# Experts' weights in transfers of 2 MB into pairs of raw slots, in place of 1 MB into one

## The chip, the core and the metric

The kernel runs on one core of a Trainium2 chip. Its engines have instruction queues of their own: TensorE (PE; its weight loads are PEld), VectorE (DVE), ScalarE (ACT), GpSimd (POOL) and SyncE (SP, which here only issues DMAs); sixteen DMA engines move data between the chip's memory (HBM) and the core's on-chip memory (SBUF, 128 partitions). Engines wait for one another by semaphores. The time is the device time of one execution in microseconds, as the median of several runs.

## The reference

The input x has 256 rows of 1024 values, all float32. Two blocks of two layers each follow one another. The part that the change touches is the mixture of experts in the second layer of the first block:

```python
def swiglu(x, w_gate, w_up, w_down):
    return (jax.nn.silu(x @ w_gate) * (x @ w_up)) @ w_down

def moe_swiglu(x, w_router, w_gate, w_up, w_down):
    logits = (x @ w_router).astype(jnp.float32)
    top_v, top_i = lax.top_k(logits, TOP_K)          # 2 of 8 experts per row
    top_w = jax.nn.softmax(top_v, axis=-1)
    gates = jnp.sum(jax.nn.one_hot(top_i, N_EXPERTS, dtype=jnp.float32) * top_w[..., None], axis=-2)
    out = jnp.zeros_like(x)
    for e in range(N_EXPERTS):
        out = out + gates[..., e:e + 1] * swiglu(x, w_gate[e], w_up[e], w_down[e])
    return out
```

Each expert has w_gate and w_up of 1024 x 3584 and w_down of 3584 x 1024. The other three layers have attention or a gated delta rule, and dense gated feed-forward parts.

## The kernel before

All weights come as a stream of units. A unit is 128 partitions x 2048 float32, 1 MB, 8 KB in each partition, and lies in HBM as one contiguous block. The stages of a unit are:

1. SyncE issues its DMA into one of six slots of `raw` (`RAW = 6`, line 41), slot `i % RAW` for unit number i. Before the issue it waits until VectorE has done with the unit that was in the slot, number i - 6.
2. ScalarE rounds it into `w_hi` (float32r, `split_hi`, line 521). It waits for the landing of the unit (`wait_loaded`) and for TensorE to be done with the unit three before, since `w_hi` and `w_lo` have three slots (`SPLIT = 3`).
3. VectorE takes the difference `raw - w_hi` into `w_lo` (`split_lo`, line 526) and so frees the raw slot.
4. TensorE multiplies with three products per block, w_hi x_hi, w_lo x_hi and w_hi x_lo (line 771).

A unit's slot is thus requested anew as soon as VectorE's subtraction is over. Each raw slot has a semaphore `loaded`, which a transfer raises by 16.

The expert stage is a hardware loop of eight turns, one per expert, on every engine; the units of a turn are always the same 42 (`EXPERT`, `TURN`). In a step, one for each 512 of the 3584 hidden units, there are two units of w_gate (`wu_eg`), two of w_up (`wu_eu`) and, for the hidden units of an earlier step, two of w_down (`wu_ed`); seven such steps make 42 units, with the down units shifted by two steps, so that the last six units of a turn are all of w_down. The units of one kind come in twos, numbers (f, 0) and (f, 1), and lie next to each other in HBM. The number of units of a turn is a multiple of `RAW`, so the slots are the same in each turn.

TensorE computes gate and up for 128 gathered rows, ScalarE the SiLU (line 1551), VectorE the product (line 2161), TensorE turns it (line 1055), ScalarE and VectorE make its two parts (lines 1561 and 2168), and TensorE multiplies by w_down.

On SyncE's queue stand two more transfers of 512 KB in each turn: before unit 12 (`PUT_AT`) the store of the previous expert's result `ye` to `y_by_expert` (line 588), and before unit 20 (`GET_AT`) the load of the next expert's rows `xt` (line 592). Towards the end of the stage GpSimd gathers rows of `y_by_expert` (line 676).

There is a second path (`overflow_loads`, and the tag `V`) for experts with more than 128 rows. It does not run with these inputs.

The first expert unit has number `expert_base` = 67, the first unit behind the experts has number `after` = 403, so slots are counted from an odd number. The weights for the next stage (`wu_pg`) go on in the same ring of slots.

Of the kernel before, what the change touches and what calls it, by code (L numbers as in the profile page):

```python
# [22 lines left out]
F32 = mybir.dt.float32  # L23
I32 = mybir.dt.int32
ALU = mybir.AluOpType
# [12 lines left out]
NE = 8  # L38
UNIT = 2048
WARM_START, WARM_LN, WARM_RMS = 6, 5, 4  # L40
RAW = 6
# [181 lines left out]
def build_program(nc, A, plan, debug=None):  # L223
    cst_np, cst_at = constants()
    NC = cst_np.shape[1]
    with ExitStack() as ctx:
# [230 lines left out]
            return out + down(EXP_STEPS - 1)  # L457
        EXPERT = expert_order()
        TURN = len(EXPERT)
        assert TURN % RAW == 0 and TURN % SPLIT == 0  # L460
        unit_at, n = {}, 0
        for key, arr, idx in stream_order():
            if key == ("experts",):
# [13 lines left out]
        def place(i):  # L477
            return split_no(i) % SPLIT

        def key_of(i):  # L480
# [2 lines left out]
                return expert_base + TURN + i - after  # L483
            return i

        def wait_loaded(E, eng, i):
            slot, n = i % RAW, 16 * (i // RAW + 1)
            if E.ev.turn is not None:
                n = n + E.ev.turn * (16 * TURN // RAW)
            eng.wait_ge(E.loaded[slot].sem, n)  # L490
            return raw[:, slot, :]
# [31 lines left out]
        def split_lo(E, ve, i):  # L523

            ve.wait_ge(*E.hi.at("unit", i))
            nc.vector.tensor_tensor(w_lo[:, place(i), :], raw[:, i % RAW, :], w_hi[:, place(i), :].bitcast(F32), ALU.subtract) \  # L526
                .then_inc(*E.lo.mark("unit", i))

        def ahead(E, split, eng, key, base=None):
# [21 lines left out]
        @block.sync  # L551
        def _(sp):

            def overflow_loads():
                sp.wait_ge(*flag_done.at())
                r = sp.value_load(flag_i[0:1, 0:1], min_val=0, max_val=1)
                with sp.If(r > 0):
                    sp.wait_ge(*M.put.at("last"))
                    sp.dma_start(yg_own[0, P:S, :], moe["ye"]).then_inc(*V.put.mark("first"))
                    for i in range(after, after + RAW):  # L560
                        wait_loaded(M, sp, i)
                    with sp.Fori(0, NE) as e:
                        with V.ev.loop(e):
                            sp.wait_ge(V.groups.sem, e * plan.per.get("ovf_groups", 0) + 1)
                            for j, (ekey, earr, eidx) in enumerate(EXPERT):
                                if j >= RAW:
                                    sp.wait_ge(*V.lo.at("unit", j - RAW))
                                sp.dma_start(raw[:, j % RAW, :], A[earr][e, eidx[0], eidx[1]]) \
                                    .then_inc(*V.loaded[j % RAW].mark())
                            sp.wait_ge(*V.free[1].at("ovf", "ye", 1))  # L570
                            sp.dma_start(yg_own[e, P:S, :], moe["ye"]).then_inc(*V.put.mark("own"))
                    for i, (arr, idx) in zip(range(after, after + RAW), again):
                        sp.dma_start(raw[:, i % RAW, :], A[arr][idx] if len(idx) > 1 else A[arr][idx[0]]) \
                            .then_inc(*V.loaded[i % RAW].mark("again"))
                    sp.wait_ge(*V.lo.at("again", SPLIT - 1))

            again = [(arr, idx) for key, arr, idx in stream_order() if arr and after <= unit_at[key] < after + RAW]
            sp.dma_start(Rf, A["xT"].rearrange("p c n -> p (c n)")).then_inc(*first_x.mark())
            for key, arr, idx in stream_order():
                if key == ("experts",):  # L580
                    with sp.Fori(0, NE) as e:
                        with ev.loop(e):
                            for j, (ekey, earr, eidx) in enumerate(EXPERT):
                                i = expert_base + j
                                if j == PUT_AT:
                                    sp.wait_ge(*M.dve.at("moe", "zeroed"))
                                    sp.wait_ge(*turn_before(M.free[1], "moe", "ye", 1))
                                    sp.dma_start(yg_before[e, 0:P, :], moe["ye"]).then_inc(*M.put.mark("before"))
                                if j == GET_AT:
                                    sp.wait_ge(*xg_put.at("all"))  # L590
                                    sp.wait_ge(*turn_before(M.groups, "moe", "next", "ga", 1))
                                    sp.dma_start(moe["xt"], xg_next[e, 0:P, :]).then_inc(*xt_in.mark("next"))

                                sem, v = M.lo.at("unit", expert_base + (j - RAW) % TURN)
                                sp.wait_ge(sem, v - plan.per.get("lo_ready", 0) if j < RAW else v)
                                sp.dma_start(raw[:, i % RAW, :], A[earr][e, eidx[0], eidx[1]]) \
                                    .then_inc(*M.loaded[i % RAW].mark())
                    continue
                if unit_at[key] == after + RAW:
                    sp.wait_ge(*M.free[1].at("moe", "ye", 1))  # L600
                    sp.dma_start(yg[NE * S:NE * S + P, :], moe["ye"]).then_inc(*M.put.mark("last"))
                    overflow_loads()
                    for t in range(NT):
                        sp.wait_ge(*high_in[t].at(t))
                i = unit_at[key]
                if i >= RAW:
                    old = i - RAW
                    if expert_base <= old < after:
                        old = expert_base + (old - expert_base) % TURN
                    sp.wait_ge(*(reader(M, old) if old in whole else M.lo.at("unit", key_of(old))))  # L610
                src = A[arr][idx] if len(idx) > 1 else A[arr][idx[0]]
                sp.dma_start(raw[:, i % RAW, :], src).then_inc(*M.loaded[i % RAW].mark())
            for t in range(NT):
                sp.wait_ge(*x_ready.at(3, "ffn", t))
                sp.dma_start(A["out"][t * P:(t + 1) * P, :], X[:, t, :]).then_inc(*stored.mark(t))
            sp.wait_ge(*stored.last())
# [116 lines left out]
        def _(pe):  # L733
# [560 lines left out]
            for L in range(2):  # L1294
                if L == 0:
                    pe.wait_ge(*consts.at())
                    keep_warm(WARM_START, 6)
                    pe.wait_ge(*xs_ready.at("first"))
                mixer(L)
                turn_tile((L, "mix"), 0, lambda t: x_ready.at(L, "mix", t))  # L1300
                keep_warm(WARM_LN, 6)
                turn_tile((L, "mix"), 1, lambda t: x_ready.at(L, "mix", t))
                if L == 0:
                    dense_ffn(0)
                else:
                    router()
                    gather(M, "moe", "first")
                    pe.wait_ge(*flag_done.at())
                    r = pe.value_load(flag_i[0:1, 0:1], min_val=0, max_val=1)
                    gathered(M, "moe", "first")  # L1310
                    with pe.Fori(0, NE) as e:
                        with ev.loop(e):
                            experts(M, "moe", expert_base)
                    with pe.If(r > 0):
                        with pe.Fori(0, NE) as e:
                            with V.ev.loop(e):
                                experts(V, "ovf", 0)
                        for h in range(2):
                            pe.wait_ge(*V.free[h].at("ovf", "ye", h))
                        pe.wait_ge(*V.lo.at("again", SPLIT - 1))  # L1320
                        for i in range(after, after + RAW):
                            pe.wait_ge(*V.loaded[i % RAW].at("again"))

                embedding_gate(L)
            for L in range(2, 4):
# [21 lines left out]
        def _(ac):  # L1347
# [351 lines left out]
            for L in range(2):  # L1699
# [22 lines left out]
                else:  # L1722
# [20 lines left out]
                    with ac.If(r > 0):  # L1743
# [2 lines left out]
                                experts(V, "ovf", 0)  # L1746
                        ac.wait_ge(*V.groups.at("ovf", "dn", EXP_STEPS - 1))
                        for i in range(after, after + RAW):
                            ac.wait_ge(*V.loaded[i % RAW].at("again"))
                        for i in range(SPLIT):  # L1750
                            nc.scalar.copy(w_hi[:, place(after + i), :], raw[:, (after + i) % RAW, :]) \
                                .then_inc(*V.hi.mark("again", i))
                    want_root()
                    norm_root(L, "ffn", 0)
# [58 lines left out]
        def _(ve):  # L1813
# [602 lines left out]
            for L in range(2):  # L2416
# [38 lines left out]
                else:  # L2455
# [15 lines left out]
                    with ve.If(r > 0):  # L2471
# [6 lines left out]
                        for i in range(SPLIT):  # L2478
                            u = after + i
                            ve.wait_ge(*V.hi.at("again", i))  # L2480
                            V_.tensor_tensor(w_lo[:, place(u), :], raw[:, u % RAW, :], w_hi[:, place(u), :].bitcast(F32), ALU.subtract) \
                                .then_inc(*V.lo.mark("again", i))

                    def take_rows(t, nb):
# [177 lines left out]
```

## Time and profile before

| | |
|---|---|
| median of 3 runs | 2253.78 us (2248.89 to 2256.55) |
| the profiled execution | 2255.73 us, span of its instructions 2253.9 us |
| TensorE busy in the span | 2183.6 us (97%) |
| VectorE, ScalarE busy | 1699.0 us (75%), 1385.0 us (61%) |
| moved by the weight queue of SyncE | 545.82 MB in the whole program |
| expert loop | about 500 to 1440 us of the span |

The numbers of the profile come from one execution. "Busy" counts the time in which an engine executes; TensorE's matmuls overlap and their ends are modelled. "Waited for" names what ended an engine's idle time. The rows below are given as the profile has them, grouped by view.

### The profile page before, as it was taken

The numbers are of one execution on the slowest core, as the hardware profiler recorded it, in microseconds if no ns is written. First come the engines' busy times: TensorE is split into PE (matmuls) and PEld (weight loads), VectorE is DVE, ScalarE is ACT, GpSimd is POOL, SyncE is SP. The second block draws the span as 40 slices with busy tenths as digits, with TensorE's granted clock in tenths as the row PEclk, the third lists the DMA queues.
The fourth block names the chain that finished last, engine by engine and source line by source line (L and its number), as shares of the span: only waits on it lengthen the run. The fifth ranks groups of instructions, "written<-read, shape, count | busy, mean of one in ns | idle before, by whom it ended". The sixth has DMA issues, their size and how long they took to land.

```text
span 2253.9 us, 32351 instructions
## 1 busy us (share of the span) xinstructions
PE 2183.6 (97%) x12324; PEld 1870.6 (83%) x12324; DVE 1699.0 (75%) x1888; ACT 1385.0 (61%) x1455; POOL 56.6 (3%) x72
## 2 busy tenths in 40 slices
PE   8899999889999999999999999989999999999998
PEld 6699997668888888888888887769979998988998
DVE  5745457768888888888888889857677777776766
ACT  5543334647777777787777777646465446555444
POOL 2000000020000000000000003000000000000000
PEclk9999999989999999999999999989999999999999
DMA  9555555349999999999999999834135554233551
GB/s 388 217 198 185 187 182 181 119 160 386 373 384 374 385 370 386 374 372 383 366 391 360 395 358 395 327 142 155 68 122 199 178 190 147 93 122 135 184 189 55
DMA packets 81800, 573.35 MB, mean 254 GB/s; under 512 B 9553, under 2 KB 9665, under 8 KB 15985
## 3 DMA queue, kind: packets, MB, share of 16 engines
q1 hardware_dynamic: 76320, 545.82, 64.3%
q0 software_dynamic: 5376, 26.12, 3.1%
q8 instruction: 70, 1.15, 0.2%
q14 instruction: 34, 0.27, 0.0%
HBM read 564.03 MB, written 17.83 MB: 258 GB/s over the span
## 4 chain that ended last, share of the span: by engine, by line
PE 87%; DVE 5%; ACT 5%; issue 2%; DMA 1%; ACTq 0%; DVEq 0%; POOLq 0%
PE bank L771 78%; ACT w_hi L521 2%; DVE w_lo L526 2%; PE bank L1055 1%; PE bank L1180 1%; PE bank L1190 1%; ACT arena L1390 1%; PE bank L1095 1%; DVE R L1885 1%; PE bank L749 1%; PE bank L766 1%; PE bank L835 0%; PE bank L827 0%; DVE arena L1905 0%; DMA cst<-in_cst 0%
## 5 line engine op out<-in xcount | busy, mean ns | idle before, releaser
L526 DVE TENSOR_TENSOR w_lo<-raw,w_hi 128x2048 fp32r<-128x2048 f32 x508 | 1163.8, 2301 | 358.5 <-ACT w_hi L521 357.0
L521 ACT CAST w_hi<-raw 128x2048 fp32r<-128x2048 f32 x508 | 969.6, 1912 | 471.2 <-PE bank L771 465.5
L771 PE MATMUL bank<-w_hi,xT_hi 128*128 128x512 f32 x1184 | 471.5, 398 | 8.8 <-DVE xT_lo L1843 3.2
L771 PE MATMUL bank<-w_lo,xT_hi 128*128 128x512 f32 x1184 | 464.1, 392 | 0.0
L771 PE MATMUL bank<-w_hi,xT_lo 128*128 128x512 f32 x1184 | 464.1, 392 | 0.0
L771 PE MATMUL bank<-xT_hi,w_hi 128*128 128x256 f32 x1344 | 381.4, 284 | 4.5 <-DVE xT_lo L1843 3.2
L771 PE MATMUL bank<-xT_hi,w_lo 128*128 128x256 f32 x1344 | 381.1, 284 | 0.0
L771 PE MATMUL bank<-xT_lo,w_hi 128*128 128x256 f32 x1344 | 381.0, 283 | 0.0
L771 PE MATMUL bank<-w_hi,aT_hi 128*128 128x512 f32 x864 | 343.8, 398 | 3.2 <-DVE w_lo L526 3.2
L771 PE MATMUL bank<-w_lo,aT_hi 128*128 128x512 f32 x864 | 336.9, 390 | 0.0
L771 PE MATMUL bank<-w_hi,aT_lo 128*128 128x512 f32 x864 | 336.8, 390 | 0.0
L771 PEld LDWEIGHTS bank<-w_hi,xT_hi 128*128 128x128 f32 x1184 | 224.1, 189 | 66.0 <-DVE w_lo L526 9.6
L771 PEld LDWEIGHTS bank<-w_hi,xT_lo 128*128 128x128 f32 x1184 | 224.0, 189 | 48.0
L771 PEld LDWEIGHTS bank<-xT_hi,w_hi 128*128 128x128 f32 x1344 | 258.4, 192 | 6.2 <-issue 5.0
L771 PEld LDWEIGHTS bank<-w_lo,xT_hi 128*128 128x128 f32 x1184 | 224.3, 189 | 44.6 <-issue 0.5
L771 PEld LDWEIGHTS bank<-xT_lo,w_hi 128*128 128x128 f32 x1344 | 258.4, 192 | 1.1
L771 PEld LDWEIGHTS bank<-xT_hi,w_lo 128*128 128x128 f32 x1344 | 258.4, 192 | 0.0
L771 PEld LDWEIGHTS bank<-w_hi,aT_hi 128*128 128x128 f32 x864 | 162.4, 188 | 37.5 <-DVE w_lo L526 4.8
L771 PEld LDWEIGHTS bank<-w_hi,aT_lo 128*128 128x128 f32 x864 | 162.2, 188 | 35.0
L771 PEld LDWEIGHTS bank<-w_lo,aT_hi 128*128 128x128 f32 x864 | 162.6, 188 | 30.4
L1515 ACT ACTIVATE arena<-bank,fcw 128x256 f32<-128x256 f32 x88 | 44.9, 561 | 61.2 <-PE bank L771 61.2
L1551 ACT ACTIVATE arena<-bank 128x512 f32<-128x512 f32 x56 | 33.6, 599 | 42.7 <-PE bank L771 42.6
(326 smaller groups left out, 1610.7 us busy)
## 6 DMA issues: line engine op xcount, KB each, us to landing
raw<-in_wu_eg SPq DMA_DIRECT2D x112, 1024.0 KB, 7.2
raw<-in_wu_eu SPq DMA_DIRECT2D x112, 1024.0 KB, 7.1
raw<-in_wu_ed SPq DMA_DIRECT2D x112, 1024.0 KB, 7.3
raw<-in_wu_up SPq DMA_DIRECT2D x44, 1024.0 KB, 4.8
raw<-in_wu_ffn_gu SPq DMA_DIRECT2D x28, 1024.0 KB, 4.9
raw<-in_wu_in SPq DMA_DIRECT2D x28, 1024.0 KB, 4.8
raw<-in_wu_down SPq DMA_DIRECT2D x22, 1024.0 KB, 4.8
raw<-in_wu_ffn_d SPq DMA_DIRECT2D x14, 1024.0 KB, 4.8
```

The lines of the kernel that those rows point to most:

```text
L521: nc.scalar.copy(w_hi[:, place(i), :], src).then_inc(*E.hi.mark("unit", i))
L526: nc.vector.tensor_tensor(w_lo[:, place(i), :], raw[:, i % RAW, :], w_hi[:, place(i), :].bitcast(F32), ALU.subtract) \
L749: mm = nc.tensor.matmul(dst, src, diag[:, t, :], start=True, stop=True)
L766: nc.tensor.matmul(bank[b][:, :], ident, cst[:, 0:512], start=True, stop=True)
L771: mm = nc.tensor.matmul(o, l[i], r[j], start=(first and n == 0), stop=(last and n == 2), skip_group_check=not lone)
L1055: mm = nc.tensor.transpose(o[:, c * P:(c + 1) * P], moe["h"][:, f % 2, c * P:(c + 1) * P], ident)
L1095: return lambda dst, h: nc.tensor.matmul(dst, lhs(h), rhs(h), start=True, stop=True)
L1180: of_level(n, "X", t, t, lambda dst, i: nc.tensor.matmul(dst, dn["LT"][:, i, :], dn["D"][:, i, :], start=True, stop=True))
L1190: of_level(n, "D", t, 2 + t, lambda dst, i: nc.tensor.matmul(dst, dn["DT"][:, i, :], dn["Xl"][:, i, :], start=True, stop=True))
L1390: ins = nc.scalar.activation(att["pr"][:, i, e, a:b], att["s"][:, i, e, a:b], ACT.Exp, bias=nmax[:, i, e, q:q + 1], scale=-1.0, accum_out= ...
L1515: ins = nc.scalar.activation(buf[:, s % 2, m, :], bank[b + half][:, m * S:(m + 1) * S], ACT.Identity, bias=fcw[:, c, 3:4], scale=fcw[:, c, ...
L1551: nc.scalar.activation(moe["sg"][:, f % 2, :], bank[b][:, :], ACT.Silu).then_inc(*E.free[b].mark(tag, "sg", f))
```

## The change

In the expert loop SyncE issues one DMA for two units, 2 MB, into two neighbouring slots. The pairs are units (j, j+1) with even j, which are the two halves (f, 0) and (f, 1) of one weight block. Slots are now counted by `slot_of(i) = (i + expert_base) % RAW`, so that the first expert unit has an even slot. The pair raises the semaphore of the even slot alone. ScalarE's `wait_loaded` waits for this semaphore for both units; for later stages the counts of the odd slots are reduced by what the loop no longer gives them. The first two units behind the loop (`after`, `after + 1`) come in one pair too. Before a pair, SyncE waits until VectorE has freed the second of the two slots. The overflow path keeps its single transfers.

```diff
+        def slot_of(i):
+            return (i + expert_base) % RAW
+
         def wait_loaded(E, eng, i):
-            slot, n = i % RAW, 16 * (i // RAW + 1)
+            slot, n = slot_of(i), 16 * (i // RAW + 1)
+            if E is M and i >= expert_base and (i - expert_base) % 2:
+                if i < after + 2:
+                    eng.wait_ge(E.loaded[slot - 1].sem, 16 * ((i - 1) // RAW + 1) + (E.ev.turn * (16 * TURN // RAW) if E.ev.turn is not None else 0))
+                    return raw[:, slot, :]
+                n -= 16 * (NE * TURN // RAW + (slot == slot_of(after + 1)))
...
                             for j, (ekey, earr, eidx) in enumerate(EXPERT):
                                 i = expert_base + j
-                                if j == PUT_AT:
+                                if j % 2:
+                                    continue
+                                if j == PUT_AT - PUT_AT % 2:
...
-                                sem, v = M.lo.at("unit", expert_base + (j - RAW) % TURN)
+                                sem, v = M.lo.at("unit", expert_base + (j + 1 - RAW) % TURN)
                                 sp.wait_ge(sem, v - plan.per.get("lo_ready", 0) if j < RAW else v)
-                                sp.dma_start(raw[:, i % RAW, :], A[earr][e, eidx[0], eidx[1]]) \
-                                    .then_inc(*M.loaded[i % RAW].mark())
+                                sp.dma_start(raw[:, slot_of(i):slot_of(i) + 2, :], A[earr][e, eidx[0], :, :, :].rearrange("i p n -> p i n")) \
+                                    .then_inc(*M.loaded[slot_of(i)].mark())
...
+                if i == after + 1:
+                    continue
+                if i == after:
+                    sp.wait_ge(*M.lo.at("unit", expert_base + (old + 1 - expert_base) % TURN))
+                    sp.dma_start(raw[:, slot_of(i):slot_of(i) + 2, :], A[arr][idx[0], 0:2, :, :].rearrange("i p n -> p i n")) \
+                        .then_inc(*M.loaded[slot_of(i)].mark())
+                    continue
```

Elsewhere `i % RAW` becomes `slot_of(i)`. No instruction is moved on TensorE, VectorE or ScalarE.

On SyncE's queue before, around the store of ye in each turn (eu is w_up, ed is w_down, lo_ready counts VectorE's subtractions):

```order
L596 DMA raw<-in_wu_eu 128x2048 [waits lo_ready]
L595 REGISTER_ALU
L596 DMA raw<-in_wu_eu 128x2048 [waits lo_ready]
L587 REGISTER_ALU [waits dve_step]
L588 ISA [waits free1]
L588 DMA y_by_expert<-arena 128x1024
L595 REGISTER_ALU
L596 DMA raw<-in_wu_ed 128x2048 [waits lo_ready]
L595 REGISTER_ALU
L596 DMA raw<-in_wu_ed 128x2048 [waits lo_ready]
```

And the same place now:

```order
L608 DMA raw<-in_wu_eu 128x2x2048 [waits lo_ready]
L598 REGISTER_ALU [waits dve_step]
L599 ISA [waits free1]
L599 DMA y_by_expert<-arena 128x1024
L606 REGISTER_ALU
L608 DMA raw<-in_wu_ed 128x2x2048 [waits lo_ready]
```

Two issues with a wait each have become one issue with one wait, and the store stands between the same units as before.

At the end of the loop and behind it (pg, pp and in are the next stages' weights), before:

```order
L596 DMA raw<-in_wu_ed 128x2048 [waits lo_ready]
L581 REGISTER_ALU
L581 COMPARE_AND_BRANCH
L612 DMA raw<-in_wu_pg 128x2048 [waits lo_ready] x3
L612 DMA raw<-in_wu_pp 128x2048 [waits lo_ready]
```

And now:

```order
L608 DMA raw<-in_wu_ed 128x2x2048 [waits lo_ready]
L591 REGISTER_ALU
L592 COMPARE_AND_BRANCH
L627 DMA raw<-in_wu_pg 128x2x2048 [waits lo_ready]
L631 DMA raw<-in_wu_pg 128x2048 [waits lo_ready]
L631 DMA raw<-in_wu_pp 128x2048 [waits lo_ready]
```

The first two of the three pg units came one by one and come as a pair now; behind them all is as it was.

## Rows read from the trace of the kernel before

**Rows 1.** The page: busy times, and the chain that ended last by engine.

```profile
PE 2183.6 (97%) x12324; PEld 1870.6 (83%) x12324; DVE 1699.0 (75%) x1888; ACT 1385.0 (61%) x1455; POOL 56.6 (3%) x72
...
PE 87%; DVE 5%; ACT 5%; issue 2%; DMA 1%; ACTq 0%; DVEq 0%; POOLq 0%
```

**Rows 2.** Busy time in a stretch of the loop; columns in the first row.

```profile
core 0: us, PE busy (x) PEld busy (x) DVE busy (x) ACT busy (x) POOL busy (x), PEclk, DMA share, GB/s
640.00:740.00 100.00, 99.99 (x458) 82.66 (x457) 86.94 (x49) 75.54 (x52) 0.00 (x0) 1.00 0.97 379
```

**Rows 3.** Waits from 520 to 1440: waiter, awaited, us, times, longest.

```profile
ACT w_hi L521 <- PE bank L771: 170.4, 241, 2.5
...
PEld bank L771 <- DVE w_lo L526: 11.3, 29, 1.8
...
PE bank L771 <- DVE w_lo L526: 3.5, 8, 1.4
```

**Rows 4.** Waits of SyncE's queue in the whole program.

```profile
SPq L596 <- DVE w_lo L526: 851.4, 336, 31.8
```

**Rows 5.** Timeline of SyncE: start, time to the last one's end, merged.

```profile
925.28 3.40 SPq L596 DMA_DIRECT2D raw<-in_wu_eg  x2
930.93 3.05 SPq L596 DMA_DIRECT2D raw<-in_wu_eu  x2
```

**Rows 6.** Timeline of ScalarE: start, duration, idle before and its cause.

```profile
920.75 1.91 ACT L521 CAST w_hi<-raw 128x2048 fp32r<-128x2048 f32 x1 [0.81 <-PE bank L771]
...
923.94 1.92 ACT L521 CAST w_hi<-raw 128x2048 fp32r<-128x2048 f32 x1 [0.79 <-PE bank L771]
926.66 1.92 ACT L521 CAST w_hi<-raw 128x2048 fp32r<-128x2048 f32 x1 [0.80 <-PE bank L771]
...
937.54 1.91 ACT L521 CAST w_hi<-raw 128x2048 fp32r<-128x2048 f32 x1 [0.81 <-PE bank L771]
```

**Rows 7.** Timeline of VectorE, the subtraction behind the cast of 920.75.

```profile
922.82 2.29 DVE L526 TENSOR_TENSOR w_lo<-raw,w_hi 128x2048 fp32r<-128x2048 f32 x1
```

**Rows 8.** Landing of the one raw transfer issued in 408:409, us.

```profile
DMA to landing us min/median/max: 4.7/4.7/4.7
```

**Rows 9.** Timeline of SyncE, the gate and up pairs at 1368 to 1378.

```profile
1368.94 3.39 SPq L596 DMA_DIRECT2D raw<-in_wu_eg  x2
1374.99 3.46 SPq L596 DMA_DIRECT2D raw<-in_wu_eu  x2
```

**Rows 10.** Landing of the raw transfer issued at 1372.00, window 1372:1372.5.

```profile
DMA to landing us min/median/max: 11.5/11.5/11.5
```

**Rows 11.** Landing of the raw transfer issued at 1374.99, window 1374.5:1375.5.

```profile
DMA to landing us min/median/max: 11.0/11.0/11.0
```

**Rows 12.** Landing of all raw transfers issued in 520:1440.

```profile
DMA to landing us min/median/max: 5.1/7.2/12.4
```

**Rows 13.** Timeline of SyncE around a store of ye.

```profile
1102.52 3.65 SPq L596 DMA_DIRECT2D raw<-in_wu_eu  x2
1106.43 0.36 SPq L588 DMA_DIRECT2D y_by_expert<-arena  x1
```

**Rows 14.** Landing of the raw transfer in the window 1105.5:1106.

```profile
DMA to landing us min/median/max: 8.8/8.8/8.8
```

**Rows 15.** Timeline of ScalarE, the cast of the unit issued at 1102.52.

```profile
1114.45 1.91 ACT L521 CAST w_hi<-raw 128x2048 fp32r<-128x2048 f32 x1 [0.81 <-PE bank L771]
```

**Rows 16.** Timeline of GpSimd, the gather.

```profile
1356.69 1.56 POOL L676 DMA_INDIRECT arena<-y_by_expert,y_rows  x1 [851.62 <-issue]
```

**Rows 17.** Timeline of ScalarE, the cast of the unit issued at 1368.94.

```profile
1381.24 1.90 ACT L521 CAST w_hi<-raw 128x2048 fp32r<-128x2048 f32 x1 [0.85 <-PE bank L771]
```

**Rows 18.** Timeline of SyncE at the start of the loop.

```profile
505.57 4.04 SPq L596 DMA_DIRECT2D raw<-in_wu_eu  x2
```

**Rows 19.** Timeline of ScalarE, the cast of the unit issued at 505.57.

```profile
517.87 1.91 ACT L521 CAST w_hi<-raw 128x2048 fp32r<-128x2048 f32 x1 [0.81 <-PE bank L771]
```

**Rows 20.** Costliest groups in 520:1440: busy us, mean ns, idle before.

```profile
L526 DVE TENSOR_TENSOR w_lo<-raw,w_hi 128x2048 fp32r<-128x2048 f32 x324 | 742.7, 2306 | 110.3 <-ACT w_hi L521 109.1
```

More of the change, by code:

```diff
@@ L459, in build_program @@
         TURN = len(EXPERT)
-        assert TURN % RAW == 0 and TURN % SPLIT == 0
+        assert TURN % RAW == 0 and TURN % SPLIT == 0 and RAW % 2 == 0
         unit_at, n = {}, 0
@@ L525, in split_lo @@
             ve.wait_ge(*E.hi.at("unit", i))
-            nc.vector.tensor_tensor(w_lo[:, place(i), :], raw[:, i % RAW, :], w_hi[:, place(i), :].bitcast(F32), ALU.subtract) \
+            nc.vector.tensor_tensor(w_lo[:, place(i), :], raw[:, slot_of(i), :], w_hi[:, place(i), :].bitcast(F32), ALU.subtract) \
                 .then_inc(*E.lo.mark("unit", i))
@@ L567, in overflow_loads @@
                                     sp.wait_ge(*V.lo.at("unit", j - RAW))
-                                sp.dma_start(raw[:, j % RAW, :], A[earr][e, eidx[0], eidx[1]]) \
-                                    .then_inc(*V.loaded[j % RAW].mark())
+                                sp.dma_start(raw[:, slot_of(j), :], A[earr][e, eidx[0], eidx[1]]) \
+                                    .then_inc(*V.loaded[slot_of(j)].mark())
                             sp.wait_ge(*V.free[1].at("ovf", "ye", 1))
@@ L572, in overflow_loads @@
                     for i, (arr, idx) in zip(range(after, after + RAW), again):
-                        sp.dma_start(raw[:, i % RAW, :], A[arr][idx] if len(idx) > 1 else A[arr][idx[0]]) \
-                            .then_inc(*V.loaded[i % RAW].mark("again"))
+                        sp.dma_start(raw[:, slot_of(i), :], A[arr][idx] if len(idx) > 1 else A[arr][idx[0]]) \
+                            .then_inc(*V.loaded[slot_of(i)].mark("again"))
                     sp.wait_ge(*V.lo.at("again", SPLIT - 1))
@@ L588, in _ @@
                                     sp.dma_start(yg_before[e, 0:P, :], moe["ye"]).then_inc(*M.put.mark("before"))
-                                if j == GET_AT:
+                                if j == GET_AT - GET_AT % 2:
                                     sp.wait_ge(*xg_put.at("all"))
@@ L592, in _ @@
                                     sp.dma_start(moe["xt"], xg_next[e, 0:P, :]).then_inc(*xt_in.mark("next"))
-                                sem, v = M.lo.at("unit", expert_base + (j - RAW) % TURN)
+                                sem, v = M.lo.at("unit", expert_base + (j + 1 - RAW) % TURN)
                                 sp.wait_ge(sem, v - plan.per.get("lo_ready", 0) if j < RAW else v)
-                                sp.dma_start(raw[:, i % RAW, :], A[earr][e, eidx[0], eidx[1]]) \
-                                    .then_inc(*M.loaded[i % RAW].mark())
+                                assert EXPERT[j + 1] == (EXPERT[j][0][:-1] + (1,), earr, (eidx[0], 1)) and eidx[1] == 0
+                                sp.dma_start(raw[:, slot_of(i):slot_of(i) + 2, :], A[earr][e, eidx[0], :, :, :].rearrange("i p n -> p i n")) \
+                                    .then_inc(*M.loaded[slot_of(i)].mark())
                     continue
@@ L610, in _ @@
                     sp.wait_ge(*(reader(M, old) if old in whole else M.lo.at("unit", key_of(old))))
+                if i == after + 1:
[5 more added lines that the diff above has]
+                    continue
                 src = A[arr][idx] if len(idx) > 1 else A[arr][idx[0]]
-                sp.dma_start(raw[:, i % RAW, :], src).then_inc(*M.loaded[i % RAW].mark())
+                sp.dma_start(raw[:, slot_of(i), :], src).then_inc(*M.loaded[slot_of(i)].mark())
             for t in range(NT):
@@ L1321, in _ @@
                         for i in range(after, after + RAW):
-                            pe.wait_ge(*V.loaded[i % RAW].at("again"))
+                            pe.wait_ge(*V.loaded[slot_of(i)].at("again"))
                 embedding_gate(L)
@@ L1748, in _ @@
                         for i in range(after, after + RAW):
-                            ac.wait_ge(*V.loaded[i % RAW].at("again"))
+                            ac.wait_ge(*V.loaded[slot_of(i)].at("again"))
                         for i in range(SPLIT):
-                            nc.scalar.copy(w_hi[:, place(after + i), :], raw[:, (after + i) % RAW, :]) \
+                            nc.scalar.copy(w_hi[:, place(after + i), :], raw[:, slot_of(after + i), :]) \
                                 .then_inc(*V.hi.mark("again", i))
@@ L2480, in _ @@
                             ve.wait_ge(*V.hi.at("again", i))
-                            V_.tensor_tensor(w_lo[:, place(u), :], raw[:, u % RAW, :], w_hi[:, place(u), :].bitcast(F32), ALU.subtract) \
+                            V_.tensor_tensor(w_lo[:, place(u), :], raw[:, slot_of(u), :], w_hi[:, place(u), :].bitcast(F32), ALU.subtract) \
                                 .then_inc(*V.lo.mark("again", i))
```

## The prediction

> **What bounds the kernel now.** I read the busy times and the chain first. TensorE is busy 2183.6 of 2253.9 us, and 87% of the chain that ended last is TensorE, 1% is DMA [rows 1]. The change touches one stage only, the loop over the eight experts, so a stretch of that stage comes next: from 640 to 740 TensorE is busy 99.99 of 100 us at a granted clock of 1.00, and the DMA share is 0.97 at 379 GB/s [rows 2]. Two resources look full there. Which of them holds the other up, the waits tell. From 520 to 1440 ScalarE's cast waited 241 times for TensorE (it wants the w_hi slot back), 170.4 us in all, and never for a landing. TensorE waited 3.5 us and its weight loads 11.3 us for the subtraction [rows 3]. On the other side SyncE waited 336 times, 851.4 us in all, for VectorE to free a raw slot [rows 4]. So the raw weights stand ready before they are wanted, and TensorE sets the pace: one unit (1 MB, twelve matmuls) each 2.72 us, the distance of the casts at 923.94 and 926.66 [rows 6].
>
> **What is removed.** 336 issues become 168. Each keeps SyncE's queue for some 0.36 us (the one of 512 KB that stands alone took that [rows 13]). SyncE is on no one's path here, so this is worth 0. The landing that is waited for comes from DMA work, and that is not less: the bytes are the same.
>
> **What is added: a wait of one unit more, and a longer transfer.** The pair is issued when the second of its two slots is free, so the first half leaves as late as the second did. In the steady pattern the gate pair's second issue begins at 925.28+3.40-0.36 = 928.32 [rows 5], and the pair's first cast at 937.54 [rows 6]: 9.2 us. The up pair's second issue is at 930.93+3.05-0.36 = 933.62, 5.3 us behind. I take the gate pair for the tightest of a step's three.
>
> After the cast's present start there is more cover. Cast and subtraction of one unit end at 922.82+2.29 = 925.11 [rows 7], 4.36 us after the cast began at 920.75 [rows 6]. The cast begins as TensorE frees the slot, and TensorE then has two more units, 5.44 us. So 1.08 us of lateness costs TensorE nothing. If that cover is absent, each late microsecond counts.
>
> Queued behind a late cast on ScalarE are the SiLU and the copy of the turned hidden units, behind them VectorE's product, and TensorE's transposes wait for that; SyncE's next issue waits for the subtraction. All of them have the same microsecond of room, since ScalarE idles 0.80 us before most casts [rows 6].
>
> How long does a 2 MB transfer take? No row has one. Below: a lone 1 MB lands in 4.7 us [rows 8], and two transfers issued into a long queue, at 1372.00 and 1374.99, land at 1383.5 and 1386.0 [rows 9, 10, 11], 2.5 us apart, so the second MB costs 2.5 and the pair 7.2 us. Above: the usual landing in the loop is 7.2 us [rows 12], because each transfer finds one ahead of it; with the second MB that makes 9.7 us. Both are inside 9.22+1.08 = 10.3 us. I take the middle, 8.5 us, since the two rows are equally near: the pairs leave some 5.3 us apart and find less ahead of them. So the undisturbed pairs cost 0.
>
> The Trainium skill (DMA: Bandwidth & Descriptors, section Anatomy of one DMA) gives, for transfers issued by GpSimd, a fit of 2.0 us plus the bytes at 436 GB/s, and from it follows that larger transfers are cheaper; by it a pair lands in 6.8 us (an estimate), no pair is ever late, and the sum below would be 0. The lone landing of 4.7 us [rows 8] agrees roughly with it (4.4); the 7.2 us of the loop [rows 12] do not.
>
> **The disturbed places.** Twice per expert SyncE puts 512 KB in between (the store of ye, the load of xt).
> - Store of ye, for the sixth expert: the second up half left at 1102.52+3.65-0.36 = 1105.8 and landed 8.8 us later, at 1114.6, and the store was issued at 1106.43 [rows 13, 14]. The first cast of the pair stands at 1114.45 [rows 15], with cover 1115.5. Kept as before, that is 0.9 us early. But the first half can no longer flow in the 3.3 us before: if the queue would have been empty then, its 2.5 us come on top and the pair is 1.6 us late; if it was never empty, nothing is added. Between 0 and 1.6 I take 0.4 us, because a landing of 8.8 shows a queue that is mostly not empty. The load of xt, eight units later, meets what is left of this queue; I count one late pair per expert for both. Eight experts: 3 us (bounds 0 and 13).
> - GpSimd's gather of the finished experts' rows, from 1356.69 on [rows 16], with the load of xt behind: the second gate half lands at 1383.5 [rows 9, 10], the first cast is at 1381.24 [rows 17], with cover 1382.3. That is 1.2 us late already, as long as all else stands; I take 2 us, as the carried queue grows a little (bounds 1.2 and 1.2+2.5 = 3.7).
> - Start of the stage: the second of the two up halves leaves at 505.57+4.04-0.36 = 509.25 and its pair's first cast is at 517.87 [rows 18, 19], 8.6 us, the shortest of all. With cover 9.7 us, so 0 (bounds 0 and 0).
>
> At the stage's end the pair of pg units follows the same pattern, so 0.
>
> **Sum.** 0 + 3 + 2 = 5 us. The profiled execution took 2255.73 us (span 2253.9), so it would take 2260.7; it stands 1.95 us above the median of 2253.78. Against the median: 2258.7 us. Less than 0 has no term: no engine waits for a landing in this stage, so nothing is there to win by landing sooner. The upper bound of these terms is 13+3.7, some 17 us.
>
> **Rivals.**
> 1. The queue does not thin out and the cover is not there. Then each of the 56 steps (seven per expert) has its gate pair 9.7-9.2 = 0.5 us late: 28 us, and with a part of the disturbed places 16 to 30 us; time 2270 to 2284, I say 2276. For it: the DMA share is 0.97 already [rows 2], so what is pushed back is made up slowly. Against: a stall delays the following issues too, which thins the queue. It decides where pairs land more than 10.3 us after their issue.
> 2. The pair reads badly. Each partition now takes 8 KB from one block and 8 KB from another 1 MB further on. The loop draws 379 GB/s [rows 2]; should this pattern bring a fifth less, the loop is DMA bound and its 920 us (520 to 1440) grow to 920/0.8 = 1150, time about 2480. Against: only the order of the pieces changes, and each stays 8 KB. [...]
> 3. Faster. TensorE's 3.5 us and its weight loads' 11.3 us of waiting for w_lo [rows 3] go away, as fewer transfers write beside ScalarE's and VectorE's reading of raw. That gives at most 15 us: 2239. Against: the subtraction takes 2306 ns on the mean of the stage [rows 20], and 2.29 us where it runs alone in step [rows 7], so there is nothing in it to speed up.
> 4. All hidden: every pair within its budget, 0 us, 2253.8.
>
> **Chances.** Within 0.3% (6.8 us, about what this measurement can tell from none): forecast and rival 4, 0.53 together, the forecast alone 0.33 and rival 4 0.20. Slower: 0.40, being the forecast's own terms at their upper bounds 0.12, rival 1 0.25, rival 2 0.03. Faster, rival 3 or the scatter of the medians: 0.07. The range for 8 of 10 goes from 2249, the scatter of no change, to 2283, rival 1 nearly whole. The forecast's own range is 2252 to 2266.
>
> **What would show it.** Right: the casts still wait for TensorE and only a few, once or twice per expert after the stores of ye and in the gather, wait for DMA; landings of the pairs at 7.5 to 9.5 us; TensorE at 99 of 100 us. Wrong by rival 1: waits of the cast for raw in every step, and 16.8 us per step grown to 17.3. Wrong by rival 2: landing beyond 11 us everywhere. Wrong by rival 3: w_lo waits gone.

## The result, and the profile after

The changed kernel takes 2262.4 us (median of 11 runs, 2258.18 to 2270.9) against 2253.28 us (11 runs, 2248.89 to 2256.59): 9 us slower. The ratio over all runs is 1.005, 95% interval 1.0036 to 1.0064 (the two medians alone give 1.004). The profiled execution took 2267.89 us, span 2266.1, so it is one of the slower ones of the eleven, and the differences of its rows to those of before are 12 us and not 9.

The page of the changed kernel, busy times and chain, which answer to [rows 1]:

```profile
PE 2189.5 (97%) x12324; PEld 1866.6 (82%) x12324; DVE 1696.0 (75%) x1888; ACT 1383.7 (61%) x1455; POOL 55.3 (2%) x72
...
PE 77%; DVE 7%; ACT 7%; DMA 6%; issue 3%; ACTq 0%; DVEq 0%; SPq 0%; POOLq 0%
```

Busy times are within 6 us of those before. What is new is a chain that runs for 6% of the span, some 136 us, through DMA; it was 1%.

Stretches of the loop, against [rows 2] (columns as there); the third row is the second stretch in the kernel before:

```profile
640.00:740.00 100.00, 99.69 (x454) 81.61 (x453) 86.74 (x50) 75.57 (x52) 0.00 (x0) 1.00 0.99 381
840.00:940.00 100.00, 99.03 (x445) 79.96 (x444) 85.20 (x49) 75.35 (x53) 0.00 (x0) 1.00 0.97 372
...
840.00:940.00 100.00, 99.78 (x454) 81.82 (x453) 87.33 (x49) 77.26 (x54) 0.00 (x0) 1.00 0.98 381
```

TensorE is busy for 99.69 and 99.03 of 100 us, where it was 99.99 and 99.78, at the same granted clock of 1.00.

Waits from 520 to 1440, against [rows 3]:

```profile
DVE w_lo L535 <- ACT w_hi L530: 122.9, 151, 1.9
ACT w_hi L530 <- PE bank L790: 69.1, 115, 2.5
ACT w_hi L530 <- DMA raw<-in_wu_eg: 55.5, 34, 2.9
ACT w_hi L530 <- DMA raw<-in_wu_eu: 43.1, 31, 3.1
PEld bank L790 <- DVE w_lo L535: 26.5, 63, 1.8
ACT w_hi L530 <- DMA raw<-in_wu_ed: 15.9, 15, 1.5
PE bank L790 <- DVE w_lo L535: 8.8, 19, 1.4
```

The cast never waited for a landing; now it does 80 times, 114.5 us in all. Most of that is time in which it would have waited for TensorE anyway (170.4 us before, 69.1 now). What gets through to TensorE is small: its waits for w_lo rise from 3.5 to 8.8 us and those of its weight loads from 11.3 to 26.5 us.

Landings of the raw transfers issued in 520:1440, then of the single pair in 401:403, which had no other weight transfer beside it:

```profile
DMA to landing us min/median/max: 7.7/9.8/12.1
```

```profile
DMA to landing us min/median/max: 8.0/8.0/8.0
```

The first answers to [rows 12], 7.2 us for 1 MB; the second to [rows 8], 4.7 us. Of the 159 pairs issued in 520:1440, 36 landed more than 10.3 us after their issue, the limit that the prediction set.

SyncE's stores of ye before unit 12 stand at the same point of each turn, so their distance is the length of a turn. First and eighth, of the changed kernel:

```profile
509.85 0.39 SPq L599 DMA_DIRECT2D y_by_expert<-arena  x1
...
1355.16 0.37 SPq L599 DMA_DIRECT2D y_by_expert<-arena  x1
...
1467.75 0.35 SPq L613 DMA_DIRECT2D y_by_expert<-arena  x1
```

And of the kernel before:

```profile
509.88 0.38 SPq L588 DMA_DIRECT2D y_by_expert<-arena  x1
...
1345.06 0.36 SPq L588 DMA_DIRECT2D y_by_expert<-arena  x1
...
1454.00 0.35 SPq L601 DMA_DIRECT2D y_by_expert<-arena  x1
```

Seven turns took 845.31 us in place of 835.18, that is 1.45 us more per turn. With the last row of each (the store behind the loop) the loop's length, by which the experiments are compared below, is 957.90 us against 944.12: 13.8 us longer. So the whole loss lies in the loop; the rest of the program takes nothing of it. These are single executions, and the rest of the program differs between them too: 1309.8 us before, 1308.2 here, and down to 1301.3 in the runs below.

Where in a turn the time is lost, the first matmul of each unit tells, set beside the same matmul before (both traces have all 12324). In turns two to seven TensorE falls 8.6 us behind in all, 5.5 us of it before the first matmuls of units 10 and 12 (counted from 0 in a turn), between whose pairs the store of ye is issued; the other 3.1 us are spread over the turns. Behind the eighth store the loop took 112.59 us in place of 108.94: 3.7 us more, some 1.8 us at the store's place again and some 1.1 us in the eight units behind it, where the gather of GpSimd falls.

The place behind a store, in the seventh turn. SyncE, then ScalarE:

```profile
1232.76 0.37 SPq L608 DMA_DIRECT2D raw<-in_wu_eu  x1
1233.38 0.37 SPq L599 DMA_DIRECT2D y_by_expert<-arena  x1
1237.76 0.38 SPq L608 DMA_DIRECT2D raw<-in_wu_ed  x1
```

```profile
1237.09 3.73 ACT L530 CAST w_hi<-raw 128x2048 fp32r<-128x2048 f32 x2 [0.63 <-DMA raw<-in_wu_eg]
1243.50 1.91 ACT L530 CAST w_hi<-raw 128x2048 fp32r<-128x2048 f32 x1 [2.69 <-DMA raw<-in_wu_eu]
1245.32 0.58 ACT L1580 CAST aT_hi<-bank 128x512 fp32r<-128x512 f32 x1
...
1249.60 3.72 ACT L530 CAST w_hi<-raw 128x2048 fp32r<-128x2048 f32 x2 [1.41 <-DMA raw<-in_wu_ed]
1254.62 1.92 ACT L530 CAST w_hi<-raw 128x2048 fp32r<-128x2048 f32 x1 [1.29 <-DMA raw<-in_wu_eg]
```

The up pair left at 1232.76 and is cast at 1243.50, 10.7 us later, after ScalarE had stood idle for 2.69 us. The down pair behind the store left at 1237.76 and took 11.8 us. Cast and copy of the turned units queue behind it, as the prediction said.

### The profile page after: what moved, and what is told of

The parts are those of the page before. It is cut to its first block, busy times and chain, and to the rows that moved or that the text cites. A ratio compares the mean times of both kernels' runs of the same rounds, so it can differ in the third digit from the quotient of the medians.

```text
span 2266.1 us, 31792 instructions
## 1 busy us (share of the span) xinstructions
PE 2189.5 (97%) x12324; PEld 1866.6 (82%) x12324; DVE 1696.0 (75%) x1888; ACT 1383.7 (61%) x1455; POOL 55.3 (2%) x72
## 4 chain that ended last, share of the span: by engine, by line
PE 77%; DVE 7%; ACT 7%; DMA 6%; issue 3%; ACTq 0%; DVEq 0%; SPq 0%; POOLq 0%
PE bank L790 69%; ACT w_hi L530 4%; DVE w_lo L535 4%; DMA raw<-in_wu_eu 3%; DMA raw<-in_wu_eg 2%; PE bank L1199 1%; PE bank L1074 1%; PE bank L1209 1%; ACT arena L1409 1%; PE bank L1114 1%; DVE R L1904 1%; PE bank L768 1%; DMA raw<-in_wu_ed 1%; PE bank L785 1%; PE bank L854 0%
```

## The experiments

Theory **A**: the loss needs two things at once, that the pair is issued only when its second slot is free, and that its first half can't be used before the second has landed; the store of ye adds to it. Rivals: the late issue alone (**B**), the joint use alone (**C**), slow reading of two blocks 1 MB apart (**D**), the size of the transfer (**F**). The first four expectations (late_singles, joint_wait, pairs_contiguous, pairs_small_both) took it that this happens only where a 512 KB transfer stands; pairs_small_both refuted that, and the later ones call A2 what was made of it: each plain pair, landing some 9.7 us after its issue and wanted after 9.2, can be late too. Ratios are to the kernel before, run on the same chip, with 95% intervals.

**Late issue, separate transfers.** On the kernel before (behind the loop the first unit waits in the same way, not printed here):

```diff
-                                sem, v = M.lo.at("unit", expert_base + (j - RAW) % TURN)
-                                sp.wait_ge(sem, v - plan.per.get("lo_ready", 0) if j < RAW else v)
+                                if j % 2 == 0:
+                                    sem, v = M.lo.at("unit", expert_base + (j + 1 - RAW) % TURN)
+                                    sp.wait_ge(sem, v - plan.per.get("lo_ready", 0) if j < RAW else v)
```

> The kernel before, but in the expert loop (and for the first two units behind it) both transfers of a pair are issued when the second slot is free; they stay two transfers of 1 MB, each with its own semaphore. Theory A (a late issue costs time only together with the longer landing of one 2 MB transfer, whose first half can't be used alone): the first half lands some 7 us after its issue, inside the 9.2 us; no cast waits for DMA in the plain steps, few by the stores; 2254 us (2251 to 2257). Rival B (the wait for the second slot alone does it, since the DMA engines stand idle meanwhile and the queue behind the store grows): as the changed kernel, 2260 to 2264 us, with some 80 waits of the cast for a landing.

Measured: 2251.52 us against 2250.24, ratio 1.000 (0.9988 to 1.0012). Its waits of the cast for DMA in 520:1440 are three:

```profile
ACT w_hi L521 <- PE bank L774: 168.8, 239, 2.5
...
ACT w_hi L521 <- DMA raw<-in_wu_eu: 1.1, 1, 1.1
ACT w_hi L521 <- DMA raw<-in_wu_ed: 0.6, 1, 0.6
ACT w_hi L521 <- DMA raw<-in_wu_eg: 0.6, 1, 0.6
```

Rival B is out: the later issue alone costs nothing that shows.

**Joint use, early issue.** On the kernel before, in `wait_loaded`:

```diff
             eng.wait_ge(E.loaded[slot].sem, n)
+            if E is M and expert_base <= i < after + 2 and (i - expert_base) % 2 == 0:
+                m = 16 * ((i + 1) // RAW + 1)
+                if E.ev.turn is not None:
+                    m = m + E.ev.turn * (16 * TURN // RAW)
+                eng.wait_ge(E.loaded[(i + 1) % RAW].sem, m)
```

> The kernel before with all its issues as they were; only ScalarE, before the cast of the first unit of each pair in the expert loop, also waits for the landing of the second. Theory A: the second half lands 7.2 us after its issue and is wanted 9.2 us after it, so the joint landing alone costs only where the queue is long (by the stores and the gather), 0 to 2 us: 2253 to 2256 us. Rival B gives the same here. A rival C (joint use alone explains the loss): 2260 us or more.

Measured: 2252.07 us, ratio 0.9998 (0.9987 to 1.0010). Waits for DMA in 520:1440:

```profile
ACT w_hi L526 <- DMA raw<-in_wu_eg: 6.6, 5, 1.7
ACT w_hi L526 <- DMA raw<-in_wu_eu: 6.1, 4, 1.8
...
ACT w_hi L526 <- DMA raw<-in_wu_ed: 0.9, 2, 0.6
```

Rival C is out. The run shows the cover as well: eleven late casts with 13.6 us of waiting, and the loop is 944.46 us long (stores at 506.94 and 1451.40), 0.3 us more than before. The longest of these waits are 1.8 us, where the cast waits 0.8 us for TensorE anyway, so up to some 1 us of lateness was free.

**Both, with transfers of 1 MB.** The two edits above together.

> The kernel before with both halves of the change's timing but none of its size: both transfers of a pair are issued when the second slot is free, the first cast waits for both landings, and they stay two transfers of 1 MB each. Theory A2 (late issue and joint use together make the loss; a second half lands some 9.7 us after a late pair issue, wanted at 9.2, with 1.1 us of cover): as the changed kernel, +7 to +13 us, some 60 to 90 waits of the cast for DMA. Rival F (one DMA of 2 MB is itself slower than two of 1 MB): within 3 us of the kernel before, second halves landing below 9 us.

Measured: 2258.09 us against 2251.22, ratio 1.0035 (1.0021 to 1.0049), so the loss is there. But the profiled execution was the fastest of its twelve (2249.71 us), with 25 waits for DMA and a loop of 946.58 us, 2.5 us longer than before, and the rest of the program was 8.5 us shorter. It could not show where the 7 us are. Hence the same kernel once more:

> The same kernel as late_joint, for a second profile, since the first profiled execution was the fastest of its twelve and its median is +7 us. Theory A2: a profile of an execution near the median shows some 60 waits of the cast for DMA and a loop that is 5 to 10 us longer. Otherwise the +7 us would have to lie outside the loop.

Measured: 2257.98 us against 2252.21, ratio 1.0031 (1.0019 to 1.0044). This time the profiled span was 2261.8 us, and its waits are of the kind that the changed kernel has, 52 for DMA in place of 80 (some 60 were expected):

```profile
ACT w_hi L526 <- DMA raw<-in_wu_eg: 45.1, 27, 2.5
ACT w_hi L526 <- DMA raw<-in_wu_eu: 29.7, 20, 3.4
PEld bank L779 <- DVE w_lo L531: 25.1, 55, 1.8
...
ACT w_hi L526 <- DMA raw<-in_wu_ed: 5.3, 5, 1.7
```

The loop took 955.34 us (512.25 to 1467.59), 11.2 us longer. The second half of a pair landed 9.6 us (median) after the first was issued, where the 2 MB transfer takes 9.8; in the fast execution above it was 8.6 us. So the two conditions together make most of the loss, without any transfer of 2 MB, and at the same place: 5.5 of the 7.6 us that TensorE falls behind in turns two to seven come before units 10 and 12. Whether the size adds something stays open: 1.0031 and 1.0035 lie below the change's 1.005, and the intervals overlap. Rival F, as it was put (within 3 us of the kernel before), is out.

**The halves side by side in HBM.** On the changed kernel, the weights' layout gets `.transpose(0, 1, 3, 2, 4)`, and

```diff
-A[earr][e, eidx[0], :, :, :].rearrange("i p n -> p i n")
+A[earr][e, eidx[0], :, :, :]
```

> The changed kernel with the experts' weights laid out in HBM so that a partition's two pieces of 8 KB lie side by side (16 KB), in place of 1 MB apart. Theory A: the bytes and the landing do not depend on it; landing median 9.8 us and 2262 us (2258 to 2266). Rival D (reading alternately from two blocks 1 MB apart is slow): landing median below 9 us and 2254 to 2257 us.

Measured: 2260.43 us, ratio 1.0041 (1.0025 to 1.0057); landings in 520:1440:

```profile
DMA to landing us min/median/max: 7.4/9.6/12.2
```

9.6 us against 9.8, and most of the loss is still there: rival D is out.

**Small store and load.** On the changed kernel, which also fills the low rows of y_by_expert once before the loop (not printed here) and leaves the experts' results and rows out:

```diff
-sp.dma_start(yg_before[e, 0:P, :], moe["ye"])
+sp.dma_start(yg_before[e, 0:P, 0:8], moe["ye"][:, 0:8])
-sp.dma_start(moe["xt"], xg_next[e, 0:P, :])
+sp.dma_start(moe["xt"][:, 0:8], xg_next[e, 0:P, 0:8])
```

> The changed kernel; the store of ye and the load of xt in the expert loop move 8 columns in place of 1024 (the low rows of y_by_expert are filled once before the loop, so the experts' results and rows are left out). Theory A (the loss arises where a 512 KB transfer stands between the pairs): the jump of 1 to 2 us per expert behind the store goes, 2251 to 2255 us. Rival E (each plain step loses a little, since pairs land at 9.8 us after issue and 9.2 are wanted): the loss stays, 2259 us or more.

Measured: 2257.7 us, ratio 1.0029 (1.0016 to 1.0043), and a loop of 951.63 us (507.37 to 1459.00), 7.5 us longer than before where the change's was 13.8. Both expectations miss: the time lies between them. 59 waits of the cast for DMA are left, so the larger part of the loss does not need the 512 KB transfers. How much goes with them the times don't show: the interval overlaps that of the change (1.0036 to 1.0064) and that of pairs_contiguous on the same chip (1.0025 to 1.0057), and the loops of single executions of one kernel lie as far apart (946.58 and 955.34 us above). The place within the turn shows that they have a part: the pair in front of the store lands in 9.3 us (median of turns two to seven) in place of 10.7, the pair behind it in 10.4 in place of 11.8, and TensorE loses 1.3 us before units 10 and 12 in place of 5.5, with 2.6 in place of 3.1 us elsewhere.

**Store and load elsewhere.** On the changed kernel:

```diff
-PUT_AT, GET_AT = 12, 20
+PUT_AT, GET_AT = 8, 28
```

> The changed kernel with the store of ye before unit 8 (was 12) and the load of xt before unit 28 (was 20). Theory A2: the store now falls in the stretch at a turn's start where pairs land 1 to 2.5 us early, so the jump of 1.3 to 2 us behind it goes and the loss of the plain steps stays: +4 to +7 us over the kernel before. Rival G (the extra 512 KB cost the same wherever they stand, as the DMA engines have no reserve): as the changed kernel, +9 us.

Measured: 2257.73 us, ratio 1.0025 (1.0016 to 1.0034), within what theory A2 says, and its interval ends below that of the change. The profiled execution, 5.7 us above this kernel's median, doesn't show a gain: 79 waits of the cast for DMA, and its first eight stores are as far apart as the changed kernel's:

```profile
494.16 0.39 SPq L599 DMA_DIRECT2D y_by_expert<-arena  x1
...
1339.53 0.37 SPq L599 DMA_DIRECT2D y_by_expert<-arena  x1
```

That is 845.37 us for seven turns, against 845.31. The loss has moved, though: in turns two to seven TensorE loses 1.7 us before units 10 and 12 and 6.0 us elsewhere. So whether the place of the 512 KB matters stays open. It is no better than the kernel before.

**Which pairs.** A function tells for each unit whether it comes in a pair; the units of the other kinds are issued one by one as in the kernel before:

```diff
+        def in_pair(i):
+            if expert_base <= i < after:
+                return EXPERT[(i - expert_base) % TURN][1] in ("wu_ed",)
+            return False and after <= i < after + 2
```

and, for the other run, `("wu_eg", "wu_eu")` and `True`.

> Only the units of w_down come in 2 MB pairs; gate and up units (and the pg units) come one by one. Theory A2: a down pair is wanted 10.3 us after its issue, with cover 11.4, and lands after some 9.7: 0 to +2 us over the kernel before, few waits of a cast for DMA. Rival H (loss in proportion to the number of pairs, a third of them here): +3 us.

> Only the units of w_gate and w_up come in 2 MB pairs (and the first two pg units); down units come one by one. Theory A2: the gate pairs with 9.2 us are the tight ones and the down units now leave earlier, into the gate pairs' way no more than before: most of the loss stays, +5 to +9 us. Rival H (in proportion, two thirds): +6 us; this run alone doesn't tell them apart, together with the down units' it does.

Measured: down only 2250.4 us, ratio 0.9999 (0.9987 to 1.0011), and gate and up only 2259.83 us, ratio 1.0038 (1.0024 to 1.0053). The casts that wait for DMA are seven in the first:

```profile
ACT w_hi L543 <- DMA raw<-in_wu_ed: 6.0, 7, 1.8
```

and 59 in the second:

```profile
ACT w_hi L543 <- DMA raw<-in_wu_eg: 56.1, 29, 3.1
ACT w_hi L543 <- DMA raw<-in_wu_eu: 43.0, 30, 2.9
```

A third of the pairs costs nothing and two thirds cost 8.6 us, so the loss is not in proportion (rival H): it goes by whether a pair has the time. In the kernel before, 10.3 us lie between a down pair's second issue and its first cast, 9.2 us for a gate pair and 9.8 us for an up pair (medians); in these two runs down pairs landed in 9.3 us, gate and up pairs in 9.6 and 9.7. Whether the single units between them also leave a pair a shorter queue isn't shown.

**Half the bytes.** On the changed kernel, slots and columns cut to `0:1024`, so half of the experts' weights are left out:

```diff
-sp.dma_start(raw[:, slot_of(i):slot_of(i) + 2, :], A[earr][e, eidx[0], :, :, :].rearrange("i p n -> p i n"))
+sp.dma_start(raw[:, slot_of(i):slot_of(i) + 2, 0:1024], A[earr][e, eidx[0], :, :, 0:1024].rearrange("i p n -> p i n"))
```

> The changed kernel, but each pair transfer in the expert loop brings only the first 1024 of a unit's 2048 columns (1 MB per pair; half of the experts' weights are left out). Issue times and the joint wait stay. Theory A2: the landing falls to 5 to 6 us, far inside 9.2, so no cast waits for DMA and the time is that of the kernel before, 2249 to 2254 us. A rival K (the waits in the queues or the new slot and semaphore scheme cost something by themselves): 2258 us or more.

Measured: 2249.28 us against 2252.21, ratio 0.9983 (0.9973 to 0.9993). In 520:1440:

```profile
ACT w_hi L530 <- PE bank L790: 170.5, 242, 2.5
...
PEld bank L790 <- DVE w_lo L535: 11.4, 28, 1.8
PE bank L790 <- DVE w_lo L535: 3.7, 9, 1.4
```

```profile
DMA to landing us min/median/max: 4.7/4.9/7.9
```

No wait for DMA is left, and the loop has 943.90 us (508.26 to 1452.16). The slots, semaphores and SyncE's waits of the change cost nothing (rival K is out); its whole loss is landings that come late. The last 0.17% that this kernel is ahead of the kernel before are not explained: the loop is only 0.2 us shorter in the profiled execution, and the change touches nothing else.

## Why the prediction was right, and where not

It forecast no change or a little slower, 2258.7 us; it was 2262.4 us, within the range of 2249 to 2283. The loss of 9.1 us is nearly twice the 5 that the terms gave. It lies within the bounds of the terms (0 to 17 us) because these were wide: the terms for the plain pairs and for the store were both too small.

- **The bound.** Right. TensorE set the pace, no landing was waited for, so less than 0 had no term. Half the bytes bring the loop from 944.12 to 943.90 us.
- **Fewer issues worth 0.** Right, by the same run.
- **The mechanism.** Right: 9.2 us between a pair's issue and its first cast, some 1.1 us of cover, and a landing in between. The cover is shown by joint_wait.
- **The landing of a pair.** The value taken, 8.5 us, the middle of 7.2 and 9.7, was wrong: the median is 9.8, just above the upper bound, and both bounds were of a usual landing and left its scatter (7.7 to 12.1) out. The reason given, that pairs leaving 5.3 us apart find less ahead of them, did not hold: even pairs with no other weight transfer beside them need 7.6 to 8.6 (the four issued at 401.63, 414.60, 456.09 and 480.37).
- **The undisturbed pairs cost 0.** This step failed, by the landing. With a median of 9.8 and a scatter up to 12.1 against a limit of 10.3, a part of the plain pairs is too late: away from the store's place TensorE loses 3.1 us in six turns, some 0.5 us per turn. Without the 512 KB transfers, in which case the prediction had only these pairs and the gather left, the time is still 0.29% above before (0.16 to 0.43).
- **The store of ye.** The place was right, the term of 3 us (eight times 0.4) mis-sized, though within its bounds of 0 and 13. At the store's place TensorE loses 5.5 us in six turns, 0.9 us each, some 7 us for eight. The prediction had 9.7 us for the up pair there, cover included, and 0.4 us of lateness; the pair landed in 10.7 us. The down pair behind the store, which it did not price, landed in 11.8.
- **The gather.** The term of 2 us (bounds 1.2 and 3.7) was of the right size, if a little high: some 1.1 us behind the eighth store's place, just under the lower bound, in one execution.
- **Rivals.** Of rival 1 one condition of two came: the queue does not thin out, but the cover is there, and it is not each step that loses 0.5 us. TensorE is busy for 99.69 and 99.03 of 100 us, not for 97 (16.8 of 17.3). Rival 2 is excluded by the side-by-side layout, rival 3 by the rows of TensorE's waits, which rose. The sign of what would show it was also half right: casts waited for DMA 80 times, before about every second pair, not once or twice per expert, yet the step did not grow by 0.5 us.

## What to carry to other kernels

Where a ring of slots feeds a pipeline, count for each slot the time from "free" to "needed" and set the landing's upper end against it, not its middle. Pairing slots takes from both sides: the first slot is asked for one unit later and may be used one unit's landing later; each alone was free here, together they used up the reserve. Look at each place of the loop by itself: over half of the loss in a turn lay at one store. Here no engine waited for a landing before, so a larger transfer had nothing to give.

## What was not expected of the hardware

Four pairs issued with no other weight transfer under way took 8.0, 7.7, 8.6 and 7.6 us to land, where 1 MB took 4.7 us and the second of two queued transfers came 2.5 us behind the first [rows 8 to 11]: the second MB cost 2.9 to 3.9 us there, not 2.5. And landings differ between executions of the same program: in the kernel with both edits and 1 MB transfers the second halves landed 8.6 us (median) after the first issue in one execution and 9.6 us in another, with loops of 946.58 and 955.34 us. Its twelve executions took from 2249.71 to 2264.99 us, the 31 of the kernel before on the same chip 2245.1 to 2256.62 us. What makes the landings differ, no run shows.
